# The first layer's last six modulation units multiplied in the prompt's attention, and compression's first rounds rearranged

## The reference

```python
mod = silu(c) @ w_ada[i] + b_ada[i]      # c: 1 prompt row + 8 sample rows; 6 chunks of 1024 columns
shift_m, scale_m, gate_m, shift_f, scale_f, gate_f = split(mod, 6)
x = x + gate_m * rmsnorm(mixer(rmsnorm(x) * (1 + scale_m) + shift_m))
x = x + gate_f * rmsnorm(mlp(rmsnorm(x) * (1 + scale_f) + shift_f))
```

```python
pos_bias = einsum('rld,rlde->re', cmp_pos, w1)          # r: 0 keys, 1 values
pa = einsum('bnlrkd,rlde->bnrke', chunks, w1[:, :16])
pb = einsum('bnlrkd,rlde->bnrke', chunks, w1[:, 16:])
hidden = gelu(pa[:, :-1] + pb[:, 1:] + pos_bias)
out = einsum('bnrke,ref->bnrkf', hidden, w2)
```

## Time and profile before

| | us |
|---|---|
| runs shown, median of 3 (lowest to highest) | 2555.95 (2554.31 to 2560.63) |
| the profiled execution's own time | 2558.57 |
| its span, first to last instruction | 2556.9 |
| TensorE busy (share of the span) | 2376.5 (93%) |
| VectorE busy | 1288.4 (50%) |
| ScalarE busy | 647.3 (25%) |
| GpSimd busy | 188.9 (7%) |

### The profile page before, as it was taken

How to read it: one execution, slowest core, us unless ns; L and a number is a source line. 1 busy time by engine, 2 the same in 40 slices (tenths; PEclk the granted TensorE clock), 3 DMA queues, 4 the chain that set the end, 5 groups by cost and what they waited for, 6 DMA issues and landing times. The chain is left out here.

```text
span 2556.9 us, 45089 instructions
## 1 busy us (share of the span) xinstructions
PE 2376.5 (93%) x18670; PEld 2003.4 (78%) x18670; DVE 1288.4 (50%) x2090; ACT 647.3 (25%) x1603; POOL 188.9 (7%) x346
## 2 busy tenths in 40 slices
PE   8988788999999978999999898999999797989998
PEld 6567775699997767999888766799985686648998
DVE  2147474166552373665443286266540775535565
ACT  1101173122012342110232194121021125522200
POOL 0255000000000010000000011000004520000000
PEclk8989899899999978999999857999999897889999
DMA  9875726866544417566533255666653665293440
GB/s 348 277 241 149 234 69 198 320 240 231 215 181 146 118 42 284 211 231 231 178 132 132 69 145 167 239 224 217 244 180 97 162 206 159 63 326 124 170 172 22
DMA packets 295776, 472.72 MB, mean 185 GB/s; under 512 B 22428, under 2 KB 120749, under 8 KB 295094
## 3 DMA queue, kind: packets, MB, share of 16 engines
q1 hardware_dynamic: 265714, 432.98, 49.6%
q0 software_dynamic: 10240, 20.99, 3.1%
q10 hardware_dynamic: 19618, 15.86, 2.0%
HBM read 448.72 MB, written 38.04 MB: 190 GB/s over the span
## 5 line engine op out<-in xcount | busy, mean ns | idle before, releaser
L632 PE MATMUL PS<-hT,ring 128*128 128x132 f32 x2048 | 249.7, 277 | 6.5 <-DVE hT L757 4.2
L632 PEld LDWEIGHTS PS<-hT,ring 128*128 128x128 f32 x2048 | 238.3, 190 | 11.8 <-issue 11.0
L632 PE MATMUL PS<-mT,arena 128*128 128x132 f32 x1536 | 184.6, 276 | 0.0
L632 PEld LDWEIGHTS PS<-mT,arena 128*128 128x128 f32 x1536 | 178.7, 190 | 0.0
L2687 PE MATMUL PS<-hT,ring 128*128 128x264 f32 x768 | 172.7, 386 | 0.1
L2687 PEld LDWEIGHTS PS<-hT,ring 128*128 128x128 f32 x768 | 145.1, 190 | 24.9 <-issue 0.4
L769 DVE TENSOR_TENSOR arena<-arena,PS 128x264 f32<-128x264 f32 x224 | 89.6, 427 | 131.1 <-PE PS L632 129.9
L948 POOL DMA_DIRECT2D arena<-in_cache_nsa_kv x192 | 97.5, 508 | 497.5 <-issue 440.6
L632 PE MATMUL PS<-arena,ring 128*128 128x132 f32 x1024 | 126.9, 277 | 0.0
L632 PE MATMUL PS<-mT,ring 128*128 128x132 f32 x1024 | 125.7, 276 | 0.0
L632 PE MATMUL PS<-hT,arena 128*128 128x132 f32 x1024 | 125.7, 276 | 0.0
(11 more groups left out here) (502 smaller groups left out, 4351.9 us busy)
## 6 DMA issues: line engine op xcount, KB each, us to landing
arena<-in_w_ada SPq DMA_DIRECT2D x36, 2048.0 KB, 12.0
ring<-in_w_mlp_in SPq DMA_DIRECT2D x32, 2048.0 KB, 8.4
ring<-in_w_mlp_out SPq DMA_DIRECT2D x32, 2048.0 KB, 8.2
ring<-in_w_ada SPq DMA_DIRECT2D x12, 2048.0 KB, 19.6
ring<-in_ssd_w_in SPq DMA_DIRECT2D x12, 2048.0 KB, 8.1
ring<-in_nsa_w_in SPq DMA_DIRECT2D x10, 2048.0 KB, 9.6
ring<-in_cache_nsa_kv SPq DMA_DIRECT2D x128, 128.0 KB, 2.4
ring<-in_hg_w_in SPq DMA_DIRECT2D x8, 2048.0 KB, 7.8
```

What stands on the lines that cost most here:

```text
L632: ins = nc.tensor.matmul(PS[:, bank, at:at + HALF], lhs[:, k, p * 128:(p + 1) * 128], rhs[:, k, :], start=opens and k == 0, stop=closes an ...
```

## The change

Modulation units 6 to 11 of layer 0 leave the ring and the in-projection. The first two are loaded by SyncE at the end of compression, ahead of the key pages, into two slots of the ring; the other four in the prompt's attention, each when the unit two before it has been multiplied; the window keys, which use the same two slots, come behind them. `output(n)` multiplies late unit n (n = 0 to 5) and turns unit n - 1; ScalarE, not VectorE, copies the product and adds the bias, ahead of its output copy. In layer 0 `keep_clock` stays for the first group only. GpSimd fetches its first pages when one and three entries of the shortened `FIRST` are used.

In compression of both layers the tiles taken by pairs are 1 and 2, not 0 and 2; the values' position term becomes 16 accumulating matmuls on TensorE ahead of round 1, so its 16 VectorE operations go; `sum_weights(0)` comes before the second transpose; five `keep_clock` matmuls stand ahead of round 0.

```diff
-        FIRST = (("in", 0), ("in", 1), ("ada", 4), ("ada", 5), ("in", 2), ("ada", 6), ("ada", 7), ("in", 3), ("ada", 8),
-                 ("ada", 9), ("in", 4), ("ada", 10), ("ada", 11))
+        FIRST = (("in", 0), ("in", 1), ("ada", 4), ("ada", 5), ("in", 2), ("in", 3), ("in", 4))
+        LATE = range(6, 12)
...
-            products = {8: 4, 9: 5, 11: 6, 12: 7, 14: 8, 15: 9} if first else {}
+            products = {8: 4, 9: 5} if first else {}
...
-                for b, used in enumerate((2, 8) if first else (1, 2)):
+                for b, used in enumerate((1, 3) if first else (1, 2)):
...
-                if first:
-                    multiply(10)
...
-                if first:
-                    turn(10)
-                    multiply(11)
...
-            by_pairs = (0, 2)
+            by_pairs = (1, 2)
...
                     sp.wait_ge(product_made.sem, product_made.at(4 * cached))
+                    if l == 0:
+                        for q in LATE[0:2]:
+                            late_load(sp, q)
                     key_pages(sp, l, 2)
...
-                        pe.wait_ge(cmp_weighted.sem, cmp_weighted.at(16 * r))
-                        aux_ready.on(nc.tensor.matmul(PS[:, 3, r:r + 1], pos_terms[r], ones[:, 0:1], start=True, stop=True))
+                        if r == 0:
+                            pe.wait_ge(cmp_weighted.sem, cmp_weighted.at(0))
+                            ins = nc.tensor.matmul(PS[:, 3, 0:1], pos_terms[0], ones[:, 0:1], start=True, stop=True)
+                        else:
+                            for j in range(16):
+                                ins = nc.tensor.matmul(PS[:, 3, 1:2], w1[1][:, j, :], cmp_pos[:, L, 1, j // 4, j % 4:j % 4 + 1],
+                                                       start=j == 0, stop=j == 15)
+                        aux_ready.on(ins)
...
                     position(0)
+                    keep_clock(pe, PS[:, 5, 0:256], 5)
                     for n in range(len(order)):
                         if n == 1:
                             pe.wait_ge(loaded.sem, loaded.at(256))
+                            position(1)
...
                     turn(0)
+                    sum_weights(0)
                     turn(1)
-                    differences(0)
-                    sum_weights(0)
                     position(0)
...
-                        if 3 <= m < 7:
-                            for w in range(4 * (m - 3), 4 * (m - 2)):
-                                weight_position(v, w1[1], L, 1, w, cmp_weighted.at(w))
-                        if m == 8:
+                        if m == 5:
                             position(1)
...
+        def late_load(sp, q):
+
+
+            n = q - LATE[0]
+            if n >= 2:
+                sp.wait_ge(ada_ready.sem, ada_ready.at(n - 1))
+            w = sample_places(0)["slots"][n % 2].rearrange("p (k n) -> p k n", k=8)
+            ada_loaded[n % 2].on(sp.dma_start(w, a["w_ada"][0].rearrange("(k p) n -> p k n", p=128)[:, :, q * UC:(q + 1) * UC]), 16)
...
+                    if l == 0:
+                        for q in LATE[2:]:
+                            late_load(sp, q)
                     for x in range(2):
+                        if l == 0:
+                            sp.wait_ge(ada_ready.sem, ada_ready.at(5 + x))
...
-                            if i == 0 and g == 0:
+                            if i == 0 and g == 0 and (l or n == 0):
                                 keep_clock(pe, PS[:, 5 + x % 2, 0:256], 4)
...
+                    def late_modulation(n):
+
+
+                        if 1 <= n <= len(LATE):
+                            nc.tensor.transpose(PS[:, 7, 384:512], ada_tmp[:, :], ident)
+                        if n < len(LATE):
+                            pe.wait_ge(ada_loaded[n % 2].sem, ada_loaded[n % 2].at(16 * (n // 2)))
+                            w = d["slots"][n % 2].rearrange("p (k n) -> p k n", k=8)
+                            for kk in range(8):
+                                for m in range(4):
+                                    ins = nc.tensor.matmul(PS[32 * m:32 * m + 32, 7, 256:384], cT[:, kk, :],
+                                                           w[:, kk, m * 128:(m + 1) * 128], start=kk == 0, stop=kk == 7)
+                            ada_ready.on(ins)
...
                             pe.wait_ge(out_taken.sem, out_taken.at(n))
+                        if l == 0:
+                            late_modulation(n)
...
                         act.wait_ge(out_ready.sem, out_ready.at(n + 1))
+                        if l == 0 and 1 <= n <= len(LATE):
+                            for m in range(4 * (n - 1 + LATE[0]), 4 * (n + LATE[0])):
+                                c0 = 384 + 32 * (m % 4)
+                                nc.scalar.activation(mod[:, 0, m, :], PS[:, 7, c0:c0 + C], ACT.Identity, bias=b_ada(0, m, 1))
+                        if l == 0 and n < len(LATE):
+                            nc.scalar.activation(ada_tmp[:, :], PS[:, 7, 256:384], ACT.Copy)
                         out_taken.on(nc.scalar.activation(
```

## The result

| | before | changed |
|---|---|---|
| median, us (runs, lowest to highest) | 2556.34 (4, 2554.31 to 2560.63) | 2529.93 (4, 2529.37 to 2531.62) |
| span of the profiled execution, us | 2556.9 | 2528.7 |

The ratio of the times is 0.9906, with a 95% interval of 0.9878 to 0.9934: 17 to 31 us less. The forecast was 2529.5.

The account below looks back on a forecast made before the run. Limits: TensorE plus a weight wait in the in-projection, VectorE in early compression, SyncE's pages at its end, a ring of waits in the prompt's attention. -16.2 - 10.1 + 2.3 + 10.5 - 12.8 = -26.3, so 2529.5 us, range 2520 to 2539.

Parts of the forecast that it names:

- The likeliest case: Whole kernel: the forecast of 2529.5 us, own range 2520 to 2539, chance 0.52.
- The stall: In-projection, layer 0: weights delayed by early pages stall TensorE 5.2 us at unit 4's copy; lower clock costs 2.5 more.
- The rival in which the pages cost nothing: In-projection, layer 0: compression weights land in time despite page fetches at 64 us; 2522 us, chance 0.16.
- the waits for pages: Compression: page groups land late, but transposes' lead mostly absorbs the waits; TensorE loses 0.8, 1.1 and 0.3 us.
- the price of the position product: Compression, both layers: 32 passes on TensorE at 0.095 us each, 3.0 us.
- the forecast's 113.2: Compression, both layers: 113.2 us from first transpose to last cached product, against 123.2 and 126.0.
- pages issued meanwhile pay about 0.1 each: Late loads, end of layer 0's compression: pages issued while the 4 MB drain pay this; with issue, +2.3 us.
- The turn of 20 us: Prompt's attention, layer 0: 17 us between the long exponentials, two groups a turn, become about 20.
- late work: Prompt's attention, layer 0: the even group's unit (2.0) and odd group's ScalarE work (1.05) add 3.05 us a turn.
- the removed keep-clock calls: Prompt's attention, layer 0: removing three calls of 1.99 us gives nothing back, since TensorE waits for ScalarE's weights anyway.
- The rival in which the clock falls in the ring: Prompt's attention, layer 0: fewer keep-clock calls let the clock fall, three times losing 1.75 to 2.5; about 2536, chance 0.12.
- the ring's clock: TensorE's clock in the prompt attention's ring of waits among ScalarE, TensorE and VectorE, two groups a turn of 17.0 us.

Follow-up runs that it names:

- pages_late: The changed kernel with GpSimd's first page fetches at 3 and 5 units used, not 1 and 3; 2523.2 us, ratio 0.9873.
- move_only: The kernel before with the move of modulation units 6 to 11 alone, compression as before; 2550.86 us, ratio 0.9978.
- keep_back: The changed kernel with the three keep-clock calls of the first layer's prompt attention restored; 2532.94 us in one run.
- the timed parts: The kernel before with the compression part alone, 2535.39 us, and with all other hunks alone, 2550.86 us.
- loads_behind: The changed kernel with the first two late loads issued behind the 32 key pages, not ahead of them; 2525.71 us, ratio 0.9876.

## Why the prediction came true, and where it did not

The likeliest case came, and its mechanisms can all be seen; the agreement to 0.4 us is better than its terms.

- **In-projection.** Right in mechanism and size: -17.1 for -16.2. The stall was sized 5.2 + 2.5 and measured 3.93 + 2.71, the weights being 5.4 us late and not 6.6; pages_late shows that it is the pages, and that without it the stage is 68.3 us (67.7 forecast). The rival in which the pages cost nothing fell.
- **Compression, layer 0.** -10.4 for -10.1, from two errors that cancel: round 2 starts at 33.9 us, not 32.8 (the position product takes 3.5 us from its start to the next product's, not 3.0, and the rounds around it 12.5 and 13.0, not 12.2 and 12.8), but the waits for pages that were to cost TensorE 1.9 us cost it at most 0.25, the one wait left in its timeline. The pages land as forecast, 28.5, 55.5 and 81.3 us behind the first transpose; it is VectorE's waits for them, 3.74, 4.44 and 3.73 us, that are all eaten. (The forecast lists the three waits as 0.8, 1.1 and 0.3, which is 2.2, and adds 1.9; with its own terms the sum is 113.3 to 113.6, not 113.2.)
- **Compression, layer 3.** -9.8 for -12.8: the step that failed is the price of the position product, costed at its passes alone. It can also be followed by the lower clock in the round behind it. Where it isn't, the forecast's 113.2 is met: 112.7 to 113.9 over the ten passages without a fall. The other end of the term is not firm either. The move alone has the compression of the kernel before, and its length there is 122.8, where the kernel before has 126.0, because in that trace the clock fell once more in round 1. Stretches of before and move_only at the same place, columns as above:

```profile
2019.00:2025.00 6.00, 5.36 (x18) 4.26 (x19) 0.49 (x2) 1.21 (x3) 5.07 (x10) 0.50 0.70 191
```

```profile
2014.00:2020.00 6.00, 5.12 (x29) 4.47 (x30) 2.38 (x3) 1.61 (x4) 5.03 (x11) 1.00 0.67 184
```

  Against 122.8 the gain is 10.1 us without the fall behind the position product and 6.6 with it. That the changed kernel comes to -9.8 owes 3.2 us to the slow passage in the trace it is compared with.
- **Late loads.** Right in mechanism, too small: +5.7 for +2.3, inside the bounds of 0.8 and 11. The step was "pages issued meanwhile pay about 0.1 each": over the 32 pages it came to 24.36 - 19.77 = 4.6 us. A closer look at the same queue in the changed kernel shows where, the first eight pages and the other 24:

```profile
269.76 9.77 SPq L933 DMA_DIRECT2D ring<-in_cache_nsa_kv  x8
```

```profile
280.05 14.07 SPq L933 DMA_DIRECT2D ring<-in_cache_nsa_kv  x24
```

  In the kernel before the first eight take 4.41 and the others 14.85 us. So the whole price, 5.4 us, falls on the pages issued in the 12 us behind the first late load, close to the 11 us that the forecast gave the 4 MB to drain; in that time a page paid 0.67, not 0.1. The other 1.1 us of the +5.7 are the two loads' own issue, for 0.8 forecast.
- **Prompt's attention.** +12.6 for +10.5, inside the bounds. The turn of 20 us was 19.66, but by two errors of opposite sign: late work costs 20.99 - 17.0 = 4.0 a turn, not 3.05, and the removed keep-clock calls give back 1.33, not nothing, as long as the clock holds. Where the 0.9 a turn that the forecast missed comes from was not tried. The rival in which the clock falls in the ring came true in part, for one turn and 1.5 us; in the later traces with this attention the ring's clock held in three and fell in four.
- **What was forecast as untouched.** The terms that the change touches add up to -17.1 - 10.4 + 5.7 + 12.6 - 9.8 = -19.0 us in these two traces, 7 short of the forecast; the other 9.2 lie in stages where nothing was changed. These lengths vary from one execution to the next whatever the kernel: over the fourteen traces the first layer's samples' attention takes 72.9 to 77.8 us and the second layer's recurrence, from the issue of its state loads to that of its MLP's loads, 97 to 103 (before: 76.6 and 103.2; changed: 72.9 and 98.4). Stretches of the samples' attention, of before, changed and keep_back:

```profile
396.20:472.80 76.60, 64.69 (x472) 34.09 (x472) 28.74 (x76) 18.56 (x42) 0.00 (x0) 0.86 0.84 275
```

```profile
389.60:462.50 72.90, 62.20 (x472) 34.02 (x472) 28.73 (x76) 18.55 (x42) 0.00 (x0) 0.91 0.87 283
```

```profile
388.38:466.20 77.82, 65.19 (x472) 35.35 (x472) 28.90 (x76) 18.44 (x42) 0.00 (x0) 0.87 0.83 268
```

The granted clock goes with the length only in part: the two shortest, 72.9 and 73.2 us, have 0.91, but the longest has 0.87 and the kernel before 0.86. In the recurrence it goes with it closely: 0.78 in all six traces with 103 us, 0.86 in the two with 97. Five of these six hold parts or variants of the change, so its 103.2 is not the kernel before's alone. So the pair of profiled executions flatters the change by some of these 9 us; the timed parts, -21.3 and -5.9, show that the change as a whole is worth what was forecast within their intervals. Whether a part of the shorter untouched stages belongs to the change can't be told for certain with one trace of the kernel before.

## What to carry to other kernels

Work that is moved out of one stage is not free in the next: here the move alone gained 2 to 9.5 us in 2557, while in its trace the three stages that it touches came to nothing, and the taking of work off the engine that set the pace (VectorE in compression) gained the rest. Before a load is put ahead of others in a queue, or a fetch started earlier, look at who stands behind it on the same queue or shares its engines; both could be moved back here, for 4 to 7 us each, and still came some 20 us before they were wanted: the pages, issued to 121 us, are read at 144 in pages_late, and the first late load, issued at 286 us, is read at 307 in loads_behind. Where a sum of several terms comes out right, compare the terms one by one, and the length that each is taken from with a second trace: here three were off by 2 to 3.4 us, and stages nobody touched made up for them.

## What the runs showed of the hardware

Thirty-two matmuls of one column each, 3.63 us in which the profile counts TensorE as fully busy, can be followed by the lower clock (8 of 18 passages), at up to 3.4 us for the round behind them; 128 of them lowered it in both passages seen, and took 22.4 us instead of 14.5. Of the 32 key pages issued behind 4 MB of loads on SyncE's queue the first eight took 9.8 us to issue instead of 4.4, and the other 24 no longer than without the loads (14.1 and 14.9).
